# Inverting 64x64 triangular blocks by doubling: where the factor is transposed in each level

## The reference

```python
a_mat = beta[..., :, None] * jnp.einsum('nhcid,nhcjd->nhcij', k, k) * d_strict   # 64x64, strictly lower
rhs = jnp.concatenate([beta[..., None] * v, (beta * gam)[..., None] * k], axis=-1)
sol = lax.linalg.triangular_solve(a_mat, rhs, left_side=True, lower=True, unit_diagonal=True)
u0, w = sol[..., :dv], sol[..., dv:]
```

```python
sa = jnp.einsum('nhij,nhj->nhi', s, -kk_t)
s = s * w_t[:, :, None, :] + sa[..., None] * b_t[:, :, None, :] + v_t[..., None] * k_t[:, :, None, :]
```

## Time and profile before

| | |
|---|---|
| median of three timed runs | 1992.57 us |
| the profiled execution | 1989.61 us, its span 1987.8 us, 1.8 us around it |
| granted TensorE clock, mean | 0.957 of full speed |
| PE / PEld busy | 1702.6 us (86%) / 962.9 us (48%), 17970 instructions each |
| DVE / ACT / POOL busy | 835.2 us (42%) / 638.2 us (32%) / 242.3 us (12%) |

### The profile page before, as it was taken

The page is one execution under the profiler, slowest core; times in us unless marked ns, Lnnn a source line. Parts: engine busy times, 40 slices in busy tenths (PEclk is TensorE's granted clock), DMA queues, the critical chain, the costliest instruction groups (busy, mean ns, idle before and its releaser), DMA issues.

```text
span 1987.8 us, 44255 instructions
## 1 busy us (share of the span) xinstructions
PE 1702.6 (86%) x17970; PEld 962.9 (48%) x17970; DVE 835.2 (42%) x1522; ACT 638.2 (32%) x1218; POOL 242.3 (12%) x270
## 2 busy tenths in 40 slices
PE   5998895987778777897889779999998797799996
PEld 2444543544444444444655664354446655663452
DVE  1567524111111112376655753151357647543331
ACT  3414611000000000335534535252245426523442
POOL 0002211111111111005112100000002103000001
PEclk8998996999999999998999799999998999999998
DMA  9759015999999999611000003110211000013101
GB/s 359 262 190 301 1 50 222 367 422 425 425 425 424 424 424 422 256 65 42 4 3 2 3 4 126 43 43 32 80 43 34 4 2 2 4 65 105 43 1 42
DMA packets 75099, 307.76 MB, mean 155 GB/s; under 512 B 10908, under 2 KB 22300, under 8 KB 57888
## 3 DMA queue, kind: packets, MB, share of 16 engines
q1 hardware_dynamic: 63280, 291.98, 37.4%
q0 software_dynamic: 5360, 9.33, 1.3%
q10 hardware_dynamic: 6272, 3.81, 0.7%
HBM read 301.01 MB, written 16.52 MB: 160 GB/s over the span
## 4 chain that ended last, share of the span: by engine, by line
PE 73%; DVE 10%; another core or an unknown queue 6%; ACT 5%; issue 4%; ACTq 1%; DMA 1%; DVEq 0%; POOL 0%; POOLq 0%
PE bank L522 12%; PE bank L2323 12%; PE bank L2339 6%; PE bank L1066 6%; PE bank L572 4%; PE bank L2161 3%; PE bank L2245 3%; PE bank L1037 2%; PE bank L565 2%; PE bank L538 2%; DVE arena L1645 1%; PE bank L2185 1%; PE bank L2173 1%; ACT arena L1078 1%
## 5 line engine op out<-in xcount | busy, mean ns | idle before, releaser
L522 PE MATMUL bank<-hT,arena 128*128 128x512 f32 (+1 forms) x640 | 287.2, 604 | 3.8 <-ACTq L1079 2.4
L2323 PE MATMUL bank<-arena 128*64 128x256 f32 x1792 | 214.5, 396 | 68.4 <-remote 68.4
L2323 PEld LDWEIGHTS bank<-arena 128*64 128x64 f32 x1792 | 133.9, 142 | 159.1 <-issue 108.6
L522 PEld LDWEIGHTS bank<-hT,arena 128*128 128x128 f32 (+1 forms) x640 | 122.4, 193 | 161.4 <-issue 156.9
L2929 DVE COPY arena<-bank 128x256 f32<-128x256 f32 x32 | 13.6, 425 | 329.6 <-PE bank L2331 329.6
L2339 PE MATMUL bank<-arena 128*64 128x512 f32 x448 | 104.0, 607 | 16.3 <-remote 16.3
L2583 ACT ACTIVATE arena<-bank 128x512 f32<-128x512 f32 x32 | 19.1, 597 | 292.8 <-PE bank L2339 292.8
L1078 ACT ACTIVATE arena<-bank 128x512 f32<-128x512 f32 (+2 forms) x124 | 73.2, 590 | 117.4 <-PE bank L522 79.0
L1066 PE MATMUL bank<-arena 128*128 128x512 f32 x256 | 110.4, 593 | 0.0
L572 PE MATMUL bank<-hT,arena 128*128 128x512 f32 x224 | 106.7, 615 | 2.2 <-remote 2.2
L554 PE MATMUL bank<-arena 64*64 64x64 f32 x3200 | 75.8, 237 | 32.8 <-DVE arena L1645 15.0
(11 more groups left out here) (454 smaller groups left out, 2881.2 us busy)
## 6 DMA issues: line engine op xcount, KB each, us to landing
arena<-w_gate SPq DMA_DIRECT2D x28, 2048.0 KB, 30.5
arena<-w_up SPq DMA_DIRECT2D x28, 2048.0 KB, 21.0
arena<-w_down SPq DMA_DIRECT2D x28, 2048.0 KB, 26.3
arena<-w_ada SPq DMA_DIRECT2D x12, 2048.0 KB, 20.0
arena<-w_in SPq DMA_DIRECT2D x10, 2048.0 KB, 10.1
arena<-w_out SPq DMA_DIRECT2D x6, 2048.0 KB, 8.0
arena<-w_in SPq DMA_DIRECT2D x6, 1536.0 KB, 7.2
hT<-w_up SPq DMA_DIRECT2D x4, 2048.0 KB, 20.9
```

What stands on the lines that cost most here:

```text
L522: m = pe.matmul(bank[b][0:w, :], slot2(n)[:, k, c:c + w], hT[:, k, :], start=(k == 0), stop=(k == KD - 1))
L2323: mm = pe.matmul(bank[b][c * CAP:(c + 1) * CAP, 0:FE // 2], XT[j][:, k % 4, k // 4, :], e_slot(e_at(e, i), KD)[:, k, c * (FE // 2):(c + 1) ...
```

## The change

Signs are turned round: Y, T and the kept tile hold minus the inverse, so the set-up is one predicated copy of Bn into a kept tile of minus identity (`Y0`, one per direction, in the place of two tables that are no longer needed; ACT writes them once, in layer 0), and ACT negates where it moves the results out (`scale=-1.0` in the moves of u0 and WT; the RWKV branch's Bn is negated as it is moved) and no longer where it moves V.

T is no longer transposed by DVE in each level. PE turns its 16 blocks (`turned`, L564 of the new kernel) ahead of `across`: blocks that go to the lower 64 output partitions by a transpose, the others by a product with the identity. ACT moves the turned blocks to Y in one copy (`turned_moved`): the whole tile in level 1, the changed columns later. `y_far` and `changed_half` are gone, and `back` reads Y alone. In level 1 the turned blocks go to the free columns of the direction's own two banks, later to banks 4 to 7, so waits for these banks stand ahead of level 2. In the last level DVE transposes T into Bn once `across` has read Bn, for each direction, and the new entries are taken over there.

```diff
+            def turned(d, b, at, T):
+                T = placed(T)
+                for s in range(2):
+                    for h in range(2):
+                        cols = slice(at + (2 * s + h) * CG, at + (2 * s + h + 1) * CG)
+                        for f, g in quarters_of:
+                            o, t, one = bank[b + f][half(g), cols], T[half(f), g, s, h], ident[half(f), half(f)]
+                            m = pe.transpose(o, t, one) if g == 0 else pe.matmul(o, t, one, start=True, stop=True)
+                m.then_inc(sem(f"g_y_done{d}"), 1)
...
-                            y = Y[half(g), g, s, h] if f == g else y_far[d][half(g), cols]
-                            v = V[half(g), f, s, h]
+                            y, v = Y[half(g), f, s, h], V[half(g), f, s, h]
...
+                            if l == 2 and d == 0:
+                                for n in gam_full:
+                                    n.wait()
+                            if l == 2 and d == 1:
+                                kk_free.wait()
+                            turned(d, 2 * d if l == 1 else 4 + 2 * d, 256 if l == 1 else 0, g_T[d])
                             across(d, g_Bn[d], g_T[d]).then_inc(sem(f"g_v_done{d}"), 1)
                         for d in range(2):
-                            far_full[d].wait(2)
+                            y_full[d].wait()
                             v_full[d].wait()
...
+            def turned_moved(d, Y, l):
+                b, at = (2 * d, 256) if l == 1 else (4 + 2 * d, 0)
+                dst, src = two(Y), banks[:, b:b + 2, at:at + 256]
+                if l > 1:
+                    dst, src = renewed(dst, l - 1, 1 - d), renewed(src, l - 1, 1 - d)
+                act.activation(dst, src, ACT.Copy).then_inc(sem(f"g_y_full{d}"), 1)
...
+                        if l == 0:
+                            for y in Y0:
+                                chain(act.activation(blocks(y), over_blocks(const2("I64")), ACT.Copy, scale=-1.0))
...
-                        chain(dve.tensor_tensor(blocks(g_Y[d]), blocks(g_Bn[d]), merged(d, 0, True).bitcast(F32), ALU.mult))
-                        chain(dve.scalar_tensor_tensor(blocks(g_Y[d]), blocks(g_Y[d]), -1.0, over_blocks(const2("I64")), ALU.mult, ALU.add))
-                        dve.sem_inc(sem(f"g_y_full{d}"), 1)
-                        dve.transpose(g_T[d], g_Y[d]).then_inc(sem(f"g_t_full{d}"), 1)
+                        chain(dve.copy_predicated(blocks(Y0[d]), merged(d, 0, True), blocks(g_Bn[d])))
+                        dve.transpose(g_T[d], Y0[d]).then_inc(sem(f"g_t_full{d}"), 1)
...
                             if l < LEVELS - 1:
+                                t_done[d].wait()
                                 take_over(d, g_T[d], l, False).then_inc(sem(f"g_t_full{d}"), 1)
-                                n_t[d] += 1
-                                dve.wait_ge(sem(f"g_t_full{d}"), n_t[d])
-                                dve.transpose(g_Y[d], g_T[d]).then_inc(sem(f"g_y_full{d}"), 1)
                             else:
-                                take_over(d, g_Y[d], l, True).then_inc(sem(f"g_y_full{d}"), 1)
+                                v_done[d].wait(LEVELS - 1)
+                                chain(dve.transpose(g_Bn[d], g_T[d]))
+                        if l == LEVELS - 1:
+                            for d in range(2):
+                                t_done[d].wait()
+                                take_over(d, g_Bn[d], l, True).then_inc(sem(f"g_y_full{d}"), 1)
```

More of the change, by code:

```diff
@@ L383, in build @@
         g_k2 = g_ln.rearrange("p t c -> p (t c)")[:, 0:48].rearrange("p (k g s h) -> p k g s h", k=6, g=2, s=2)
-        y_far = [rs[:, 256 * d:256 * d + 256] for d in range(2)]
+        Y0 = [const(name) for name in ("cosA", "sinA")]
         g_Bn, g_T, g_Y = [[g_TA[:, 2 * i + d, :] for d in range(2)] for i in range(3)]
@@ L1135, in values, with product_moved @@
                 to_tokens(b, g_vtok[:, :, j * P:(j + 1) * P])
-            def product_moved(d, V, l, sign):
+            def product_moved(d, V, l):
                 c = d
-                act.activation(renewed(two(V), l, c), renewed(banks[:, 2 * d:2 * d + 2, 0:256], l, c), ACT.Copy, scale=sign)\
+                act.activation(renewed(two(V), l, c), renewed(banks[:, 2 * d:2 * d + 2, 0:256], l, c), ACT.Copy)\
                    .then_inc(sem(f"g_v_full{d}"), 1)
-            def changed_half(d, Y, l):
-                for g in range(2):
-                    dst, src = y_far[d][half(g)], Y[half(1 - g), 256 * g:256 * g + 256]
-                    if l > 0:
-                        dst, src = renewed(dst, l, 1 - d), renewed(src, l, 1 - d)
-                    act.activation(dst, src, ACT.Copy).then_inc(sem(f"y_far_full{d}"), 1)
+            def turned_moved(d, Y, l):
[4 more added lines that the diff above has]
+                act.activation(dst, src, ACT.Copy).then_inc(sem(f"g_y_full{d}"), 1)
             take(act, sem("go_act"))
@@ L1218, in act_second @@
                         values(2, 0)
-                    for d in range(2):
-                        y_full[d].wait()
-                        changed_half(d, g_Y[d], 0)
                     if ht > 0:
@@ L1241, in act_second @@
                         chain.mark(act.activation(g_u0[d][:, :, 2 * ht:2 * ht + 2, :].rearrange("p t s n -> p s t n"), pieces(bank[2 * d]),
-                                             ACT.Copy))
+                                             ACT.Copy, scale=-1.0))
                     w_done.wait()
@@ L1247, in act_second @@
                                        banks[:, 4:6, 256 * d:256 * d + 256].rearrange("p f (t n) -> p f t n", t=TT),
-                                       ACT.Copy).then_inc(sem(f"g_uw_free{d}"), 1)
-                for n in e_in + gam_args + v_done + u_done + pt_full + [w_done]:
+                                       ACT.Copy, scale=-1.0).then_inc(sem(f"g_uw_free{d}"), 1)
+                for n in e_in + gam_args + v_done + y_done + u_done + pt_full + [w_done]:
                     n.clear()
@@ L1307, in act_second @@
                         k_done.wait(2)
-                        chain(act.activation(by_head(r_Bn[d]), of_banks(6, 0), ACT.Copy))
+                        chain(act.activation(by_head(r_Bn[d]), of_banks(6, 0), ACT.Copy, scale=-1.0))
                         act.sem_inc(sem("r_bn_full"), 1)
@@ L1340, in act_second @@
                                        banks[:, 4:6, 256 * d:256 * d + 256].rearrange("p f (t n) -> p f t n", t=TT),
-                                       ACT.Copy).then_inc(sem(f"g_uw_free{d}"), 1)
-                for n in v_done + u_done + [w_done, args_full]:
+                                       ACT.Copy, scale=-1.0).then_inc(sem(f"g_uw_free{d}"), 1)
+                for n in v_done + y_done + u_done + [w_done, args_full]:
                     n.clear()
```

105 lines of the change are left out of this document (48 added, 57 removed).

## The result

| | median us | runs | ratio to before, 95% interval |
|---|---|---|---|
| before | 1992.2 (1987.5 to 1993.9) | 4 | |
| changed | 2123.9 (2116.4 to 2131.5) | 4 | 1.0665 [1.0615, 1.0715] |

The kernel became 131.7 us slower. I had forecast 2036 us, 2003 to 2075: right in sign, wrong by 88 us and outside the range. The profiled execution has a span of 2116.8 us, 129.0 longer than before.

What follows compares the result with a forecast made beforehand. The prediction took PE's instruction supply, in blocks of 256, to bound the changed kernel: 36.5 + 11 - 2.8 = +45 us, giving 2036 us. The range was 2003 to 2075 us.

Steps and rivals of the forecast that it cites:

- turning on PE: Step for the 8 transposes and 8 products added per direction and level: 0.47 us of PE, between 0.35 and 2.1.
- the row of equal shape: Trace row of a quarter-array call of 32 records before the change, taken as a turn's cost: 0.47 us of PE.
- changing between transpose and product drains the quarters: Rival: up to 16 mode changes make a turn on PE 2.1 us, a pair 6.4, the kernel 2100 us; chance 0.10.
- The blocks: PE's program arrives 256 instructions at a time, at 3.7 us each; a level of both directions (pair) then takes 5.1 us.
- 3.2 us of chain: Forecast time of one pair by its dependent steps alone (turns, across, V's move, back), in place of about 3.4 us.
- The +45 us: Forecast total: 36.5 us in six rounds, 11 in the four low-clock rounds, less 2.8 for set-up.
- Up to 0.8 us or so a turn changes nothing: Claim that a turn on PE this long stays hidden, because the instruction blocks arrive later anyway.
- the six rounds: Six of ten rounds, 113.2 us before, forecast at 149.7 us, +36.5; with 3.43 us per block, 22 blocks beyond first pairs.
- The rounds with the low clock: Four rounds partly at the lower clock level, where slow pairs hide some of the blocks: +11 us together.
- Set-up, signs, last level: Set-up with one predicated copy: -2.8 us over four RWKV rounds; turned signs and DVE's transposes in the last level: nothing.
- The chain decides: Rival: PE's instructions come early enough, so dependent steps set the pair's time; -10 us, 1980 us; chance 0.09.
- a small loss: Rival: low clock hides more blocks, or blocks are begun earlier while PE waits; +5 to +25 us, 2008 us; chance 0.08.

Runs made afterwards that it cites:

- e8: The kernel of e3 with each of the four 128 x 128 transposes of a turn replaced by a product with the identity: 2023.1 us, 1.015.
- e1: Changed kernel with every block of the turn turned by a product with the identity, none by a transpose: 2058.1 us, 1.0345.
- e2: Changed kernel with each turn reordered, first the 8 transposes, then the 8 products: 2037.3 us, 1.0243.
- e7: The kernel of e3 with PE's order in a level changed to across, turned, turned, across: 1992.1 us, 1.0003.
- e5: Changed kernel with each turn's blocks in the order transpose, product, transpose, product: 2443.9 us, 1.2257.
- e4: Kernel before with only the new set-up (kept minus identity, one predicated copy per direction, signs turned), levels as before: 1990.1 us, 1.0005.
- e6: Changed kernel with each turn as 4 transposes, 4 products, 4 transposes, 4 products: 2046.7 us, 1.0274.
- e3: Changed kernel with another block layout, each turn done as four whole 128 x 128 transposes: 1989.8 us, 0.9989.

## Why the prediction was wrong

**The step that failed** is *turning on PE*: "I take 0.47 us, the row of equal shape", between 0.35 and 2.1. A turn takes 1.92 us. The mechanism was named as a rival, *changing between transpose and product drains the quarters*, with a pair of 6.4 us and a time of 2100 us; measured are 6.38 and 2124. I gave it 0.10. The argument against it was that in the earlier trace rows the width changed as well. That argument was sound, as e8 shows: the way from quarters to the whole array costs as much between products. But it only made those rows silent on the mode; it did not make the mode cheap. A turn has 10 switches, each 0.15 to 0.17 us from start to start, with a product's second pass 0.10 us behind its first in between; 0.13 us of each is the switch's own, and the rest of the turn runs two quarters at a time, where the row I took has four. That the rival's 2.1 us a turn agrees with what was measured, 2.08 with the way into it, is partly luck: it counted 16 switches at 0.1 us. Between ends a factor of 6 apart I took the row of equal shape, which had no transposes in it.

**The blocks.** Right as a bound, as e1, e2 and e7 show: 256 instructions in 3.4 to 3.9 us in e1, and nowhere in that run eight blocks in a row in less than 3.4 us each. But they do not set the changed kernel's time. They were forecast to decide because I compared 3.2 us of chain with 5.1 of blocks; the chain is 6.38. The +45 us that I summed are about what is left when 8 of the 10 switches go and the number of instructions stays (e2: +49 on its own times before). "Up to 0.8 us or so a turn changes nothing" fits e2: with its step of 1.42, 0.47 for `across` taken off, a turn takes 0.95 us and the pair stays near the blocks' time.

Two readings of the prediction were off without moving the forecast. The 28.3 us of "issue" on L565 count the weight loads with PE; PE alone has 7.3 us in 13 places. And the six rounds have 6 x 5.5 = 33 blocks and not 22 beyond the first pairs, which at 0.27 us each gives the +33 us at the upper end of the +30 to +33 that I wrote.

The Trainium skill (Runtime: NRT & Kernel Launch, Instruction fetch mechanics) calls the crossing of a block mostly hidden. In the changed kernel the trace agrees, with no "issue" wait of PE in the level lines, since PE takes 6.38 us for 1.375 blocks; in e1, which could be faster, it does not, with pauses of 1.08 and 1.41 us in the rows above and 79 us in all.

**The rounds with the low clock.** I had +11 us for four; in the run, three rounds had a part at 0.5 and took 39.0, 36.1 and 35.9 us, and the others 30.7. The low level no longer hides anything, since the switches take longer at it: the step from turn to turn is 3.91 us at it in place of 2.55, and e5's cycle 0.64 in place of 0.43.

**Set-up, signs, last level.** Nothing measurable, and e4 says the same. The first pair of a round is 6.95 us, and its last 6.55 to the start of the products after it.

**"The chain decides" and "a small loss"** are out. The sign of the result rested on the blocks, 0.87 for slower. It came out right by the switches; e2 shows that the blocks alone would have made the kernel slower too, by 49 us. So there were two reasons for the sign, and I believed the smaller.

**The range.** Its upper end, 2075, was below the one rival that I had priced above it. With 0.10 for 2100 us, and that price itself a bound at 16 switches of 0.1 us, the range had to reach there if the rival deserved any more than its 0.10. The tell was in the case itself: the resource that the change loads most, a transpose beside a product in a quarter, was the one that no row showed.

## What to carry to other kernels

Group transposes and products on TensorE, and quarter-array work with quarter-array work: here each alternation of transposes and products on quarters took 0.43 us there and back with one or two blocks of each in it, 0.26 of them for the two switches, and the profile shows that time as busy. Before work is moved onto an engine, count its instructions as well as its time: here PE's program comes at 256 instructions in 3.4 to 3.9 us, and a chain that is already at that pace gains nothing from faster steps. When a term has no row of its own, let the range reach to its far bound.

## What the hardware showed that I had not expected

- A cycle of transposes and products on quarters takes 0.428 us with one of each (e5) and 0.437 with two of each (changed kernel), at the full clock, and 0.174 more for two more of each (e6). At the 0.5 level the cycle of e5 takes 0.64, 1.5 times and not 2.
- A pause of PE in e1 ends 1.20 to 1.57 us after a transfer of 256 instructions has ended (59 places).
- Float32 transposes of 64 x 64 in a quarter of the array run two abreast, pairs starting 0.06 to 0.08 us apart in e2. Of products on quarters four records start every 0.058 us.
- With PE "busy" for 39.71 of 40 us and 510 MATMULs in them, the granted clock was 0.50 (e5). Rounds of the changed kernel, with 857 records in 30.7 us, ran at 1.00 in seven cases of ten. Why the other three were partly at 0.5 was not settled.
- On the whole array a float32 product with the identity takes two records 0.112 us apart, a transpose one, 0.109 us from start to start. The way from quarters to the whole array costs 0.148 us and back 0.205, between products (e8) as with transposes (e3).
